# Expert stage of a two-layer backbone: the combined sums go through ACT and GpSimd into x, and the hidden activations are turned later

## The chip, the cores and the metric

One core of one Trainium2 chip. The metric is the device time in microseconds of one execution of the whole program. The names of the engines are PE (TensorE), DVE (VectorE), ACT (ScalarE), POOL (GpSimd) and SP (SyncE, which issues most of the transfers). SBUF is the on-chip memory, PSUM the memory into which PE writes.

## What is computed

One inference step with two trunk layers (DEPTH = 2) over 512 latent and 128 prompt tokens of width 1024. A layer has three token mixers with a gated merge, and then a mixture of 16 experts, which is where the change lies. In the reference:

```python
def expert_choice_ffn(h, w_router, w1, w3, w2):
    ...
    cap = CAPACITY_FACTOR * n_tok // N_EXPERTS
    xt = h.reshape(n_tok, D)
    aff = jax.nn.softmax((xt @ w_router).astype(jnp.float32), axis=-1)
    g, idx = lax.top_k(aff.T, cap)
    xe = xt[idx]
    hid = jax.nn.silu(jnp.einsum('ecd,edf->ecf', xe, w1)) * jnp.einsum('ecd,edf->ecf', xe, w3)
    ye = jnp.einsum('ecf,efd->ecd', hid, w2) * g[..., None].astype(h.dtype)
    out = jnp.zeros_like(xt).at[idx.reshape(-1)].add(ye.reshape(-1, D))
    return out.reshape(B, S, D)
...
    x = x + gate2 * expert_choice_ffn(h, p['w_router'], p['w_ff1'], p['w_ff3'], p['w_ff2'])
```

Each expert takes 64 latent and 16 prompt tokens. All is fp32. Its three weight matrices are 1024 x 1024, so the experts' weights are 16 x 12 MB per layer, and each is used once.

## The kernel before

**Chunks and units.** The experts run in eight pairs (A and B) per layer. The weights of a pair come in 24 chunks of 1 MB (128 x 4 x 512 fp32) into a ring of six slots. SP issues a load when `chunks_free` allows it (L747), and POOL counts that up (L847) once DVE has read the chunk. A chunk is worked on in two units, so a pair has 48 units, numbered 0 to 47. Eight units make a job, with its result in one of the two PSUM tensors `mm`: AF0, AF1, BF0, BF1 (hidden layer of A and B, two halves each), then AO and BO (the output products).

**Splitting a unit.** A product in fp32 is made as three products of rounded operands. For a unit, ACT rounds the weights (`w_hi<-ring`, in `hi_of_chunk`), DVE takes the rest (`w_lo<-ring,w_hi`, in `lo_of_chunk`), and PE makes two times three matmuls (in `job`, L1433). There are four buffers of `w_hi` and of `w_lo` (SPLITS = 4): ACT may begin on unit m when PE is through with unit m - 4 (`w_used`, or `mm_full` at a job's end).

**Order.** Each engine has its own program, written out by hand, tied by semaphores. ACT, DVE and POOL run over the chunks n of a pair and have other work put between them: DVE's `hidden(q)` (silu(w1 part) x w3 part, from `mm` and `tmp` to `hid`) comes after chunks 5, 9, 13 and 17; then PE turns the result (four transposes into `tp`, `turn_hidden`, L1445), ACT rounds it (`hi_of_hidden`) and DVE takes the rest (`lo_of_hidden`). `TURN_AT` gives the unit of PE ahead of which the turn stands, 10, 18, 26 and 34, and `after(unit)` the chunk after which ACT and DVE have their part. `SLOTS_AT` (20) and `ROWS_AT` (38) do the same for the tokens of the next pair: `find_slots` (L1377), POOL's `fetch` (an indirect transfer of rows, L840), and `turn_rows` (L1386). All turns share one PSUM tensor `tp`, handed on by `t_full` and `t_empty`.

**Combine and spread.** The output of a pair is added into x, scaled by gate2, during the next pair. Ahead of its units 8 to 15 PE makes one tile k of sums each, 128 x 512, by two matmuls into one of two PSUM tensors `oo` (`combine`, L1396). DVE adds tile k into x ahead of its own work for unit 12 + k (`spread`, by the helper on L1931), and gives `oo` back by `o_empty`. `combine` k + 2 waits for that. After the last pair all eight follow in a row.

**Other names.** `hot_t` is the matrix by which sums go to tokens; DVE rewrites it for the next combine after AF1's turn. `select` (DVE) compares positions for the pair after. L1492, L1923, L1927 and L1931 are the helpers `copy`, `tt`, `ts` and `stt`, so rows with these lines are told apart by their tiles. `stat<-stat,lam` is L2122, in the attention part: a two-input operation on one element per partition. L790, L792 and L796 are POOL's operations in that part.

Of the kernel before, what the change touches and what calls it, by code (L numbers as in the profile page):

```python
# [23 lines left out]
D = 1024  # L24
# [265 lines left out]
UNITS = 2  # L290
# [7 lines left out]
LAYER_USED = PAIRS * USED_PAIR  # L298
COMBINE_AT = JOB_UNITS

TURN_AT = [JOB_UNITS * (q + 1) + 2 for q in range(4)]
SLOTS_AT, ROWS_AT = TURN_AT[1] + 2, TURN_AT[3] + 4


def after(unit):
# [52 lines left out]
def build(nc, a):  # L358
    ctx = ExitStack()
    with ctx:  # L360
# [20 lines left out]
        def sem(name):  # L381
            return ctx.enter_context(nc.semaphore(name))
# [42 lines left out]
        def view(at, *shape):  # L425
# [5 lines left out]
            if len(shape) == 2:  # L431
# [108 lines left out]
        rows_stored, tokens_in, slots_ready, x_rows_in = (sem("rows_stored"), sem("tokens_in"), sem("slots_ready"),  # L540
                                                          sem("x_rows_in"))
        pool_waited = sem("pool_waited")
        xhi_ready, xe_ready = sem("xhi_ready"), sem("xe_ready")
        w_hi_ready, w_ready, w_used = sem("w_hi_ready"), sem("w_ready"), sem("w_used")
        silu_out, hid_ready, hid_hi_ready = sem("silu_out"), sem("hid_ready"), sem("hid_hi_ready")
# [90 lines left out]
        def pair_used(l, e, p):  # L636

            return l * LAYER_USED + e * USED_PAIR + (p - p // JOB_UNITS + 1)

        def t_bf0(last_pair):  # L640
            return T_BF0 - 1 if last_pair else T_BF0
# [120 lines left out]
        @block.gpsimd  # L762
        def _(pool):
            pool.sem_inc(chunks_free, RING)
            pool.sem_inc(small_free, 1)
            for s in (*mm_empty, t_empty, *o_empty):
                pool.sem_inc(s, 1)
            pool.sem_inc(ye_stored, 32)

            for l in range(DEPTH):  # L770
                def consumed(turn, n, e=None):

                    wait_mm_full(pool, l, turn, e)
                    pool.sem_inc(chunks_free, n)

                def ada_consumed(blocks):
                    for n in blocks:
                        pool.wait_ge(ada_full, n + 1)
                        pool.sem_inc(chunks_free, 2)

                if l == 0:
                    ada_consumed(range(ADA_FIRST))
                consumed(MM["da_v"] + TT - 1, 2)
                consumed(MM["da_q"] + 3, 2)
                consumed(DA_K[3], 2)

                def da_mix(i):
                    (p1, p2), _ = da_maps(i)
                    pool.wait_ge(da_weight, l * DA_N + i + 1)
                    pool.tensor_scalar(p2, p2, da_slot(i, "ratio"), 1.0, ALU.mult, ALU.mult)  # L790
                    pool.drain()
                    pool.tensor_tensor(p1, p1, p2, ALU.add).then_inc(p_mixed, 1)  # L792

                def da_square(t):
                    pool.wait_ge(da_kept, l * DA_N + DA_H * (t + 1))
                    pool.tensor_tensor(tmp[t % 2][:, 0:512], da_o[:, t, :], da_o[:, t, :], ALU.mult)\  # L796
                        .then_inc(da_squared, 1)

                for i in range(DA_N):
                    da_mix(i)  # L800
                    if i >= 5 and i % DA_H == 1:
                        da_square(i // DA_H - 1)
                da_square(PRT)
                for mb in range(2):
                    ada_consumed(gate_blocks(l, 0, mb))
                    consumed(MM["da_out"] + 8 * mb + 7, 3)
                consumed(MM["mla_in"] + 3, 2)
                consumed(SW_Q[3], 2)
                for i in range(MLA_N):

                    if i == MLA_N - TT:
                        consumed(mla_prep(MH - 1, 2), 2)
                    width = T if i % TT < LT else P
                    pool.wait_ge(ml_weight, l * MLA_N + i + 1)
                    pool.tensor_scalar(ml_p[i % 3][:, 0:width], ml_p[i % 3][:, 0:width],
                                       stat[:, 16 + i % 8:17 + i % 8], 1.0, ALU.mult, ALU.mult).then_inc(ml_scaled, 1)
                for mb in range(2):
                    ada_consumed(gate_blocks(l, 1, mb))
                    consumed(MM["mla_out"] + 8 * mb + 7, 3)
                consumed(SW_V, 2)  # L820

                for u in range(SW_PAIRS):

                    width = len(sw_tiles(u // SW_P)[0]) * P
                    pool.wait_ge(sw_weight, l * SW_PAIRS + u + 1)
                    for m in range(2):
                        last = pool.tensor_scalar(sw_p[u % 3][m][:, 0:width], sw_p[u % 3][m][:, 0:width],
                                                  sw_slot(u, "weight", m), 1.0, ALU.mult, ALU.mult)
                    last.then_inc(sw_scaled, 1)
                for mb in range(2):  # L830
                    ada_consumed(gate_blocks(l, 2, mb))
                    consumed(MM["sw_out"] + 8 * mb + 7, 3)
                consumed(MM["o"] + 3, 2)
                consumed(MM["o"] + 7, 2)


                def fetch(of):
                    pool.wait_ge(slots_ready, l * PAIRS + of + 1)
                    pool.sem_inc(pool_waited, 1)
                    pool.indirect_dma_start(x_rows, None, a["h_rows"], bass.IndirectOffsetOnAxis(slot_row, 0))\  # L840
                        .then_inc(x_rows_in, 16)

                def pair(e, last_pair=False):
                    for n in range(PAIR_CHUNKS):

                        pool.wait_ge(w_ready, pair_part(l, e, n * UNITS + UNITS - 1))
                        pool.sem_inc(chunks_free, 1)  # L847
                        if n == after(SLOTS_AT) + 1 and not last_pair:
                            fetch(e + 1)

                pool.wait_ge(rows_stored, 16 * LT * (l + 1))
                pool.dma_start(tokens, a["const"][:, CONST_COLS:]).then_inc(tokens_in, 16)
                fetch(0)
                with pool.Fori(0, PAIRS - 1) as e:
                    pair(e)
                pair(PAIRS - 1, True)

# [2 lines left out]
        def _(pe):  # L862
# [138 lines left out]
            for l in range(DEPTH):  # L1001
# [436 lines left out]
                def turn_hidden(q, turn, e):  # L1438

                    half, n = q // 2, q % 2  # L1440
                    rows_ = ROWS_OF[half]
                    pe.wait_ge(hid_ready, (l * PAIRS + e) * 4 + (q + 1))
                    wait_t_empty(pe, l, turn, e)
                    for k in range(4):
                        last = pe.transpose(tp[:, k * P:k * P + rows_],  # L1445
                                            hid[0:rows_, (4 * n + k) * P:(4 * n + k + 1) * P],
                                            ident[0:rows_, 0:rows_])
                    last.then_inc(t_full, 1)
# [41 lines left out]
        def _(act):  # L1490
# [76 lines left out]
            for l in range(DEPTH):  # L1567
# [237 lines left out]
                wait_t_full(act, l, TR["hot_p"])  # L1805
                copy(hotw_pt.rearrange("p g s -> p (g s)"), tp[:, 0:2 * P]).then_inc(t_empty, 1)

                def hi_of_chunk(n, e, last_pair=False):

                    i = AT[l, "pairs"] + n  # L1810
                    for u in range(UNITS):
                        m = UNITS * n + u
                        p = m - SPLITS
                        if p >= 0:

                            if p % JOB_UNITS == JOB_UNITS - 1:
                                wait_mm_full(act, l, job_turn(p // JOB_UNITS), e)
                            else:
# [44 lines left out]

                def pair(e, before=None, last_pair=False):
                    for n in range(2, PAIR_CHUNKS if last_pair else PAIR_CHUNKS + 2):
                        hi_of_chunk(n, e, last_pair)
                        if n == 2 and before is not None:
                            outputs(BO, before, False)
                        if n == 5:
# [51 lines left out]
        def _(dve):  # L1921
# [118 lines left out]
            for l in range(DEPTH):  # L2040
# [381 lines left out]
                        dve.drain()  # L2422
                        dve.sem_inc(ye_done, 1)

                def lo_of_chunk(n, e, before=None):
                    i = AT[l, "pairs"] + n
                    for u in range(UNITS):
                        m = UNITS * n + u
                        if before is not None and 0 <= m - SPLITS - COMBINE_AT < KT:
                            spread(m - SPLITS - COMBINE_AT, before)  # L2430
                        dve.wait_ge(w_hi_ready, pair_part(l, e, m))
                        tt(w_lo[m % SPLITS][:, :, :], chunk(i)[:, u * UK:(u + 1) * UK, :],
                           f(w_hi[m % SPLITS][:, :, :]), ALU.subtract).then_inc(w_ready, 1)
# [19 lines left out]
                def hidden(q, e, last_pair):  # L2453
# [3 lines left out]
                    n = q % 2  # L2457
                    dve.wait_ge(silu_out, (l * PAIRS + e) * 4 + (q + 1))
                    tt(hid[0:rows_, n * 512:(n + 1) * 512], mm[j % 2][0:rows_, 512:1024], tmp[n][0:rows_, 0:512],
                       ALU.mult).then_inc(mm_empty[j % 2], 1)  # L2460
                    dve.drain()  # L2461
                    dve.sem_inc(hid_ready, 1)

                def lo_of_hidden(q, e):
                    rows_ = ROWS_OF[q // 2]
# [5 lines left out]

                def pair(e, before=None, last_pair=False):
                    for n in range(2, PAIR_CHUNKS if last_pair else PAIR_CHUNKS + 2):
                        lo_of_chunk(n, e, before)
                        if n == 2 and before is not None:
                            outputs(BO, before, False)
                            dve.tensor_copy(aff_slot, aff_next)
# [6 lines left out]
                        if n == 9:  # L2484
                            hidden(AF1, e, last_pair)
                        if n == after(TURN_AT[AF1]):
                            ts(hot_t[:, :], tokens, slot_tok, ALU.is_equal)
                            lo_of_hidden(AF1, e)
                        if n == after(SLOTS_AT) and not last_pair:
# [31 lines left out]
                    pair(e, e - 1)  # L2521
                pair(PAIRS - 1, PAIRS - 2, True)
                outputs(BO, PAIRS - 1, True)
                for k in range(KT):
                    spread(k, PAIRS - 1)
                dve.drain()
# [51 lines left out]
```

## Time and profile before

| | us |
|---|---|
| timed runs, median of 3 (range) | 3376.07 (3367.52 to 3376.89) |
| profiled execution | 3354.95 |
| its span, first to last instruction | 3353.1 |
| PE busy | 2950.4 (88%) |
| DVE busy | 2173.1 (65%) |
| ACT busy | 1564.2 (47%) |
| POOL busy | 216.4 (6%) |

The mean granted TensorE clock is 0.951 of full speed. The experts of layer 0 run from 1022 us to about 1670, those of layer 1 from 2652 to about 3300. A busy PE counts matmuls from start to modelled end, and these overlap, so its share says less than the distance from one matmul to the next. In a row of a timeline the bracket tells how long the engine had been idle and what ended that; "DVEq" is DVE's instruction queue, such as a drain or a semaphore operation.

### The profile page before, as it was taken

To read this page: it belongs to the slowest core of one execution; us is meant where nothing else is said; L and a number is where in the kernel's file an instruction comes from. 1 tells how busy PE (TensorE), PEld (TensorE's weight loads), DVE (VectorE), ACT (ScalarE), POOL (GpSimd) and SP (SyncE) were. 2 spreads that over 40 slices of the span, in tenths; PEclk is the share of its full clock that TensorE was granted. 3 is DMA by queue.
4 is the path that set the end of the run, shared out by engine and by line. 5 is a ranking of instruction groups with operands and counts; after the bars stand their busy time and mean duration, and the time that the engine had idled before them with its cause. 6 is when DMAs were issued, how large, how long until landed. Compare 5 with 4: busy or idle time off the path is not lost.

```text
span 3353.1 us, 43928 instructions
## 1 busy us (share of the span) xinstructions
PE 2950.4 (88%) x15398; PEld 2141.2 (64%) x15398; DVE 2173.1 (65%) x3151; ACT 1564.2 (47%) x2258; POOL 216.4 (6%) x272
## 2 busy tenths in 40 slices
PE   6979988988977999999878898889799699999995
PEld 3767855766745666666656686567585366666663
DVE  3364445565447999999835553456762699999994
ACT  3161333132126777777543413321410477777773
POOL 0050011011000000000002300110200000000000
PEclk9989999999988999999988899999999699999996
DMA  7203200311416999999811031023013399999991
GB/s 268 82 1 111 77 27 26 127 65 51 157 72 243 327 330 321 327 330 326 284 65 57 26 137 52 1 76 114 28 38 112 117 334 321 327 326 326 330 335 55
DMA packets 280117, 564.13 MB, mean 168 GB/s; under 512 B 14040, under 2 KB 19872, under 8 KB 279328
## 3 DMA queue, kind: packets, MB, share of 16 engines
q1 hardware_dynamic: 273056, 543.33, 46.0%
q10 hardware_dynamic: 4448, 9.87, 0.8%
q0 software_dynamic: 2464, 8.91, 0.7%
q8 instruction: 97, 1.59, 0.2%
q14 instruction: 52, 0.43, 0.0%
HBM read 546.44 MB, written 15.63 MB: 168 GB/s over the span
## 4 chain that ended last, share of the span: by engine, by line
PE 65%; DVE 15%; ACT 7%; issue 5%; DVEq 4%; ACTq 2%; DMA 1%; POOL 0%; POOLq 0%; SPq 0%
PE mm L943 17%; PE mm L1433 17%; PE mm L878 11%; DVE w_lo L1923 6%; PE mm L1176 2%; DVEq L2461 2%; PE mm L975 2%; ACT w_hi L1492 2%; DVE x L1931 2%; ACTq L1861 2%; PE oo L1198 1%; PE oo L915 1%; DVE scratch L2112 1%; PE tp L1185 1%; DVE scratch L1923 1%
## 5 line engine op out<-in xcount | busy, mean ns | idle before, releaser
L1923 DVE TENSOR_TENSOR w_lo<-ring,w_hi 128x1024 fp32r<-128x1024 f32 x768 | 919.2, 1221 | 87.9 <-ACT w_hi L1492 57.7
L1492 ACT ACTIVATE w_hi<-ring 128x1024 fp32r<-128x1024 f32 x768 | 803.5, 1058 | 288.6 <-PE mm L1433 266.8
L1923 DVE TENSOR_TENSOR ring_lo<-ring,dw_hi 128x512 fp32r<-128x512 f32 (+1 forms) x168 | 113.6, 682 | 393.2 <-ACT dw_hi L1492 392.9
L1492 ACT ACTIVATE dw_hi<-ring 128x512 fp32r<-128x512 f32 (+1 forms) x168 | 103.5, 622 | 522.8 <-PE mm L943 518.3
L943 PE MATMUL mm<-h_hi,ring_lo 128*128 128x320 f32 (+1 forms) x1344 | 318.3, 318 | 20.9 <-DVE ring_lo L1923 14.4
L943 PE MATMUL mm<-h_lo,dw_hi 128*128 128x320 f32 (+1 forms) x1344 | 310.6, 313 | 0.0
L943 PE MATMUL mm<-h_hi,dw_hi 128*128 128x320 f32 (+1 forms) x1344 | 310.0, 312 | 0.0
L943 PEld LDWEIGHTS mm<-h_hi,ring_lo 128*128 128x128 f32 (+1 forms) x1344 | 225.0, 190 | 52.1 <-issue 37.3
L878 PE MATMUL mm<-scratch,ring 128*128 128x512 f32 (+3 forms) x896 | 256.5, 438 | 1.6 <-ACT scratch L1492 1.6
L943 PEld LDWEIGHTS mm<-h_lo,dw_hi 128*128 128x128 f32 (+1 forms) x1344 | 227.4, 190 | 1.1
L943 PEld LDWEIGHTS mm<-h_hi,dw_hi 128*128 128x128 f32 (+1 forms) x1344 | 226.6, 189 | 1.1
L1433 PE MATMUL mm<-w_lo,xa_hi 128*80 128x512 f32 x512 | 204.5, 399 | 15.5 <-DVE w_lo L1923 9.5
L878 PEld LDWEIGHTS mm<-scratch,ring 128*128 128x128 f32 (+1 forms) x896 | 140.9, 189 | 113.5 <-issue 111.0
L1433 PE MATMUL mm<-w_lo,xb_hi 128*128 128x512 f32 x512 | 203.8, 398 | 0.0
L1433 PE MATMUL mm<-w_hi,xa_lo 128*80 128x512 f32 x512 | 202.4, 395 | 0.0
L2008 DVE RECIPROCAL tmp<-tmp 128x640 f32<-128x640 f32 x48 | 199.3, 4153 | 3.9 <-issue 0.4
L1433 PE MATMUL mm<-w_hi,xa_hi 128*80 128x512 f32 x512 | 201.4, 393 | 0.0
L1433 PE MATMUL mm<-w_hi,xb_hi 128*128 128x512 f32 x512 | 199.7, 390 | 0.0
L1433 PE MATMUL mm<-w_hi,xb_lo 128*128 128x512 f32 x512 | 199.3, 389 | 0.0
L1492 ACT ACTIVATE scratch<-mm 16x1024 f32<-16x1024 f32 (+7 forms) x140 | 99.2, 718 | 149.2 <-PE mm L943 45.4
L878 PE MATMUL mm<-merged,ring 128*128 128x512 f32 (+1 forms) x512 | 138.8, 434 | 0.0
L1492 ACT ACTIVATE pt<-tp 128x640 f32<-128x640 f32 (+3 forms) x128 | 71.3, 557 | 106.6 <-PE tp L1271 63.3
(254 smaller groups left out, 4806.0 us busy)
## 6 DMA issues: line engine op xcount, KB each, us to landing
ring<-in_w_ff SPq DMA_DIRECT2D x384, 1024.0 KB, 6.1
ring<-in_w_ada SPq DMA_DIRECT2D x48, 1024.0 KB, 7.4
ring<-in_w_gate SPq DMA_DIRECT2D x24, 1024.0 KB, 5.7
ring<-in_w_in SPq DMA_DIRECT2D x16, 1024.0 KB, 9.4
ring<-in_w_o SPq DMA_DIRECT2D x8, 1024.0 KB, 7.5
x_spill<-x SPq DMA_DIRECT2D x2, 2560.0 KB, 12.5
ring<-in_w_br_da SPq DMA_DIRECT2D x4, 1024.0 KB, 6.3
ring<-in_w_br_mla SPq DMA_DIRECT2D x4, 1024.0 KB, 6.3
```

The costliest lines, as they stand in the source:

```text
L878: last = pe.matmul(out[:, lo:hi], lhs(n), rhs(n)[:, lo:hi], start=(n == 0), stop=(n == terms - 1))
L915: last = pe.matmul(oo[n % 2][32 * kk:32 * (kk + 1), 0:512], c_t[:, half * HALF + kk, :], chunk(i)[:, kk, :], start=(half == 0), stop=(half ...
L943: last = pe.matmul(out[0:width, lo:hi], w_, h_[:, k, lo:hi], start=(k == 0 and i == 0), stop=(k == KT - 1 and i == 2))
L975: last = pe.matmul(mm[j % 2][:, 0:width], h[:, k, t * P:(t + 1) * P], weight(c, k, c0, c0 + width), start=(k == 0), stop=(k == KT - 1))
L1176: last = pe.matmul(mm[j % 2][:, at:at + hi - lo], ml_q[hd % 2][0:MQ, t * P:(t + 1) * P], ml_k[hd % 2][0:MQ, lo:hi], start=True, stop=True)
L1433: last = pe.matmul(out[0:rows_, bank:bank + 512], a_[:, k, 0:rows_], b_[n % SPLITS][:, kk, :], start=(k == 0 and i == 0), stop=(k == KT - ...
L1492: return act.activation(out, in_, ACT.Copy, scale=scale)
L1861: act.drain()
L1923: return dve.tensor_tensor(out, in0, in1, op)
L1931: return dve.scalar_tensor_tensor(out=out, in0=in0, scalar=s, in1=in1, op0=op0, op1=op1)
L2008: dve.reciprocal(t_[:, :], t_[:, :])
L2461: dve.drain()
```

## The change

1. `spread` leaves DVE for the seven combines of a layer that fall into a following pair. ACT copies `oo`, scaled by gate2, from PSUM into one of four SBUF buffers (`spread_at`: `tmp[2]`, `rstd`, two parts of `merged`), ahead of its own wait for unit 12 + k. POOL then gives `oo` back and adds the buffer into x, ahead of its wait for that chunk. The eight adds after the last pair stay on DVE, which waits for POOL's first.
2. The hidden activations are turned two units later (12, 20, 28, 36), and `find_slots` with them (22); `turn_rows` stays at 38.
3. `hidden` no longer drains: it raises `hid_ready` itself, and PE gives `mm` back at the turn.
4. DVE waits for the last combine before it rewrites `hot_t`.

```diff
@@ constants
-TURN_AT = [JOB_UNITS * (q + 1) + 2 for q in range(4)]
-SLOTS_AT, ROWS_AT = TURN_AT[1] + 2, TURN_AT[3] + 4
+TURN_AT = [JOB_UNITS * (q + 1) + 4 for q in range(4)]
+SLOTS_AT, ROWS_AT = TURN_AT[1] + 2, TURN_AT[3] + 2
+SPREADS = (PAIRS - 1) * KT
+        def spread_at(k):
+            return (tmp[2][:, 0:NLAT], rstd[:, 0:NLAT], flat[:, D:D + NLAT], flat[:, D + NLAT:2 * D])[k % 4]
@@ pool
+            pool.sem_inc(spread_done, 4)
...
+                def spread(k, of):
+                    pool.wait_ge(spread_in, l * SPREADS + of * KT + (k + 1))
+                    pool.sem_inc(o_empty[(OO["pairs"] + k) % 2], 1)
+                    pool.tensor_tensor(x[:, k, 0:NLAT], x[:, k, 0:NLAT], spread_at(k), ALU.add).then_inc(spread_done, 1)
-                def pair(e, last_pair=False):
+                def pair(e, before=None, last_pair=False):
                     for n in range(PAIR_CHUNKS):
+                        if before is not None:
+                            for m in (UNITS * n, UNITS * n + 1):
+                                if 0 <= m - SPLITS - COMBINE_AT < KT:
+                                    spread(m - SPLITS - COMBINE_AT, before)
                         pool.wait_ge(w_ready, pair_part(l, e, n * UNITS + UNITS - 1))
                         pool.sem_inc(chunks_free, 1)
@@ tensor, turn_hidden
                     pe.wait_ge(hid_ready, (l * PAIRS + e) * 4 + (q + 1))
+                    pe.sem_inc(mm_empty[job_turn(q) % 2], 1)
                     wait_t_empty(pe, l, turn, e)
@@ scalar
+                def spread(k, of):
+                    j = OO["pairs"] + k
+                    act.wait_ge(spread_done, l * SPREADS + of * KT + (k + 1))
+                    wait_o_full(act, l, j, of)
+                    copy(spread_at(k), oo[j % 2][:, :], mod[:, 40 + k, 0:1]).then_inc(spread_in, 1)
@@ scalar, hi_of_chunk
+                            if before is not None and 0 <= p - COMBINE_AT < KT:
+                                spread(p - COMBINE_AT, before)
                             if p % JOB_UNITS == JOB_UNITS - 1:
@@ vector, lo_of_chunk
-                        if before is not None and 0 <= m - SPLITS - COMBINE_AT < KT:
-                            spread(m - SPLITS - COMBINE_AT, before)
                         dve.wait_ge(w_hi_ready, pair_part(l, e, m))
@@ vector, hidden
-                       ALU.mult).then_inc(mm_empty[j % 2], 1)
-                    dve.drain()
-                    dve.sem_inc(hid_ready, 1)
+                       ALU.mult).then_inc(hid_ready, 1)
@@ vector, pair
                         if n == after(TURN_AT[AF1]):
+                            if before is not None:
+                                wait_o_full(dve, l, OO["pairs"] + KT - 1, before)
                             ts(hot_t[:, :], tokens, slot_tok, ALU.is_equal)
@@ vector, after the last pair
+                dve.wait_ge(spread_done, (l + 1) * SPREADS + 4)
                 for k in range(KT):
                     spread(k, PAIRS - 1)
```

## Rows read from the trace of the kernel before

**Rows 1.** The page: busy tenths in 40 slices of 83.8 us each, DVE and DMA.
```profile
DVE  3364445565447999999835553456762699999994
...
DMA  7203200311416999999811031023013399999991
```

**Rows 2.** Busy time by window, one pair: length, engines (instructions), PEclk, DMA share, GB/s.
```profile
core 0: us, PE busy (x) PEld busy (x) DVE busy (x) ACT busy (x) POOL busy (x), PEclk, DMA share, GB/s
...
1298.04:1377.10 79.06, 74.69 (x338) 53.82 (x337) 72.42 (x79) 59.45 (x65) 1.31 (x1) 1.00 0.93 327
```

**Rows 3.** The page: DMA issues, the experts' weights: count, KB each, us to landing.
```profile
ring<-in_w_ff SPq DMA_DIRECT2D x384, 1024.0 KB, 6.1
```

**Rows 4.** Chain of waits, 1200 to 1300 us: start, length, what, so many matmuls.
```profile
1232.43 8.20 PE mm L1433 x36
```

**Rows 5.** Timeline of PE: start, length, operation, [idle before it and who ended it]; 1270 to 1340.
```profile
1274.69 0.45 PE L1433 MATMUL mm<-w_lo,xa_hi 128*80 128x512 f32 x1 [0.69 <-DVE w_lo L1923]
...
1282.07 0.50 PE L1396 MATMUL oo<-hot_t,ye_lo 128*128 128x512 f32 x1 [0.72 <-DVE x L1931]
...
1297.55 0.49 PE L1445 MATMUL tp<-const,scratch 80*128 80x80 f32 x4 [1.11 <-DVEq L2461]
...
1310.79 0.65 PE L1445 MATMUL tp<-const,scratch 128*128 128x128 f32 x4 [0.54 <-DVEq L2461]
...
1322.76 0.65 PE L1445 MATMUL tp<-const,scratch 128*128 128x128 f32 x4 [0.33 <-DVEq L2461]
...
1339.00 0.50 PE L1433 MATMUL mm<-w_lo,hidb_hi 128*128 128x512 f32 x1 [0.87 <-DVE w_lo L1923]
```

**Rows 6.** Timeline of PE in pair 0 of the first layer.
```profile
1048.80 0.50 PE L1445 MATMUL tp<-const,scratch 80*128 80x80 f32 x4 [1.06 <-DVEq L2461]
...
1060.81 0.49 PE L1445 MATMUL tp<-const,scratch 80*128 80x80 f32 x4 [0.52 <-DVEq L2461]
```

**Rows 7.** Groups by shape, 1040 to 1640: count, busy us, mean ns, idle us before.
```profile
L1492 ACT ACTIVATE w_hi<-ring 128x1024 fp32r<-128x1024 f32 x369 | 386.5, 1058 | 136.9 <-PE mm L1433 126.5 <-issue 9.6
...
L1931 DVE SCALAR_TENSOR_TENSOR x<-oo,mod,x 128x512 f32<-128x512 f32 x56 | 41.6, 744 | 1.5 <-issue 1.4
...
L1841 ACT ACTIVATE tmp<-mm 128x512 f32<-128x512 f32 x16 | 9.3, 579 | 0.0
...
L1377 PEld LDWEIGHTS tp<-scratch 128*128 128x128 f32 x56 | 6.8, 191 | 3.3 <-issue 3.3
```

**Rows 8.** Timeline of DVE, from unit 6's w_lo to AF1's hida_lo.
```profile
1273.41 6.90 DVE L1923 TENSOR_TENSOR w_lo<-ring,w_hi 128x1024 fp32r<-128x1024 f32 x6 [0.20 <-ACT w_hi L1492]
...
1292.43 0.76 DVE L1923 TENSOR_TENSOR scratch<-const,pos_t 128x256 f32<-128x256 f32 x2
...
1295.56 1.22 DVE L1923 TENSOR_TENSOR w_lo<-ring,w_hi 128x1024 fp32r<-128x1024 f32 x1
...
1299.87 0.48 DVE L1927 TENSOR_SCALAR hot_t<-merged,stat 128x512 fp32r<-128x512 f32 x1
...
1300.26 0.48 DVE L1923 TENSOR_TENSOR hida_lo<-tp,hida_hi 128x320 fp32r<-128x320 f32 x1
```

**Rows 9.** Groups by shape, POOL, whole run: two-input operations.
```profile
L792 POOL TENSOR_TENSOR scratch<-scratch 128x640 f32<-128x640 f32 x32 | 49.5, 1546 | 5.8 <-issue 1.7
...
L796 POOL TENSOR_TENSOR tmp<-scratch 128x512 f32<-128x512 f32 x10 | 10.4, 1039 | 6.6 <-DVEq L2131 6.5
...
L792 POOL TENSOR_TENSOR scratch<-scratch 128x128 f32<-128x128 f32 x8 | 3.6, 454 | 1.2
```

**Rows 10.** Timeline of POOL and DVE side by side, 196 to 199 and 1876 to 1878.
```profile
196.38 1.54 POOL L792 TENSOR_TENSOR scratch<-scratch 128x640 f32<-128x640 f32 x1
...
196.39 0.82 DVE L2112 CUSTOM_DVE_ANT_0 scratch<-mm,const 128x640 f32<-128x640 f32 x1 [0.23 <-issue]
...
198.67 0.22 DVE L1931 SCALAR_TENSOR_TENSOR stat<-stat,lam 128x1 f32<-128x1 f32 x1
...
1876.69 1.04 POOL L796 TENSOR_TENSOR tmp<-scratch 128x512 f32<-128x512 f32 x1 [1.17 <-DVEq L2131]
...
1876.95 0.80 DVE L1931 SCALAR_TENSOR_TENSOR stat<-stat,lam 128x1 f32<-128x1 f32 x1
```

More of the change, by code:

```diff
@@ L542, in build @@
         pool_waited = sem("pool_waited")
+        spread_in, spread_done = sem("spread_in"), sem("spread_done")
         xhi_ready, xe_ready = sem("xhi_ready"), sem("xe_ready")
@@ L853, in _ @@
                 fetch(0)
-                with pool.Fori(0, PAIRS - 1) as e:
-                    pair(e)
-                pair(PAIRS - 1, True)
+                pair(0)
+                with pool.Fori(1, PAIRS - 1) as e:
+                    pair(e, e - 1)
+                pair(PAIRS - 1, PAIRS - 2, True)
         @block.tensor
@@ L1806, in _, with hi_of_chunk @@
                 copy(hotw_pt.rearrange("p g s -> p (g s)"), tp[:, 0:2 * P]).then_inc(t_empty, 1)
-                def hi_of_chunk(n, e, last_pair=False):
+                def spread(k, of):
[3 more added lines that the diff above has]
+                    copy(spread_at(k), oo[j % 2][:, :], mod[:, 40 + k, 0:1]).then_inc(spread_in, 1)
+                def hi_of_chunk(n, e, before=None):
                     i = AT[l, "pairs"] + n
@@ L1865, in pair @@
                     for n in range(2, PAIR_CHUNKS if last_pair else PAIR_CHUNKS + 2):
-                        hi_of_chunk(n, e, last_pair)
+                        hi_of_chunk(n, e, before)
                         if n == 2 and before is not None:
@@ L2423, in outputs, with lo_of_chunk @@
                         dve.sem_inc(ye_done, 1)
-                def lo_of_chunk(n, e, before=None):
+                def lo_of_chunk(n, e):
                     i = AT[l, "pairs"] + n
@@ L2473, in pair @@
                     for n in range(2, PAIR_CHUNKS if last_pair else PAIR_CHUNKS + 2):
-                        lo_of_chunk(n, e, before)
+                        lo_of_chunk(n, e)
                         if n == 2 and before is not None:
```

## Prediction

> **What bounds the kernel now.** The page is read first for its slices. In the two stretches where the experts run, DMA and DVE both show 9 almost throughout, so neither can be ruled out by eye [rows 1]. The busy time by window is read next. Over one whole pair of experts, 79.06 us, PE is busy 74.7 us, DVE 72.4, ACT 59.5, POOL 1.3, and the DMA share is 0.93 [rows 2]. A pair moves 24 chunks, and each lands 6.1 us after its issue (median) [rows 3], while the ring of six chunks turns in 6/24 x 79.06 = 19.8 us: the transfers have slack, and what is left is PE and DVE.
>
> The timeline of PE shows who holds whom. The chain of waits gives the pace of an undisturbed PE: 36 matmuls in 8.20 us, 0.228 each [rows 4]. A unit of six is 1.37 us, and 1.82 with the two matmuls of combine. So a pair's 288 + 16 matmuls cost 69.3 us. Of the other 9.8 us some 4 are transposes and find_slots, and the rest are stalls, the same six in each pair [rows 5] and small ones. I give each as the idle time printed plus some 0.15 to 0.25 us of restart: unit 4, 0.9 (DVE late behind the output of the pair before); combine 2, 1.0 (waits for DVE's add into x); AF1's transposes, 1.35; BF0's, 0.7; BF1's, 0.5 (these three wait for the drain behind `hidden`); unit 44, 1.1 (ACT and DVE late behind outputs). In pair 0 there is no combine, and AF0's and AF1's transposes wait 1.2 and 0.7 us [rows 6].
>
> **The change part by part.**
>
> *DVE loses eight adds.* Each was 0.744 us [rows 7], so 8 x 0.744 = 6.0 us of 72.4 per pair. In that phase DVE is PE's neighbour: 1.15 us for a w_lo back to back (6.90 for six [rows 8]) + 0.74 for an add = 1.9 at most, and PE needs 1.82. It is DVE's insertions there (hidden, hida_lo, the selection) that make combine 2 and AF1 late.
>
> *ACT gains eight copies.* The nearest row is the silu of the same 128x512 PSUM operand, 0.58 us [rows 7]: 4.6 us per pair onto 59.5. 1.06 for a w_hi + 0.58 = 1.64 is under 1.82, and the copy stands before the wait for w_used, in ACT's idle time. Cost nothing; if PE came faster than 1.64 per unit it would cost up to 0.3 us per unit.
>
> *Turns move two units later, and the drain behind hidden goes.* hid_ready is then 2 x 1.37 = 2.7 us less urgent, more than any of the waits. AF0 to BF1 stop stalling. find_slots moves with AF1's turn (its distance stays 2), and POOL's fetch with it by one chunk: 16 units less two remain before turn_rows, and 20 us hide it. turn_rows stays, now 2 units behind BF1's turn: the distance that find_slots has before, where PE idles 3.3/7 = 0.5 us [rows 7] with one operation more of DVE in between (hot_t, 0.48). I put 0 (range 0 to 0.5). mm_empty is given by PE at the turn, four units before its next use: nothing.
>
> *The wait of POOL.* Each add stands ahead of POOL's wait for a chunk, and behind the previous one. SP's loads are queued behind chunks_free. A delay there of a few us lies inside the ring's 19.8 - 6.1 us. But o_empty for combine 4 now comes only after POOL has passed w_ready of unit 13: PE waits for POOL, and POOL for DVE.
>
> *The adds themselves on POOL.* Not shown before. By L792, which adds two different operands: 640 elements 1.546 us, 128 elements 0.454, so 2.13 ns per element, and 512 give 1.27 us. L796 with one operand twice took 1.04 [rows 9]. I take 1.27, as the adds have two operands; ends 1.04 and 1.55. Eight are 10.2 us per pair.
>
> *What they do to DVE.* This decides the case. At 1876.95 DVE begins `stat<-stat,lam` 128x1, which has two tensor inputs in SBUF. It takes 0.80 us instead of 0.22, and ends at 1877.75; POOL's add ran from 1876.69 to 1877.73. An operation of DVE with one input in PSUM, begun at 196.39 under a POOL add that began at 196.38, takes its usual 0.82 [rows 10]. So a DVE operation with two SBUF inputs stands still until POOL's is over, and the others do not. w_lo<-ring,w_hi has two SBUF inputs, 48 times per pair; the add taken from DVE had one. No row shows a POOL operation started under such a DVE operation. Its wait is between 0 and 1.22 us. What is held by one until its last moment I read as held by one at a time, both ways, and take the upper end. The Trainium skill says the same (SBUF — State Buffer, Who interferes with whom): a DVE instruction with two SBUF inputs contends with a GpSimd instruction that reads SBUF, and the later of the two fully blocks; by it the sum below stays as it is, at 3395. The trace agrees for DVE behind POOL (0.80 against 0.22 us); no row shows the other direction.
>
> *The sum for one pair with combine* (clock of the pair shown, DVE in [rows 8]). The first POOL add can begin at 1280.7, when lo of unit 11 is done (1273.41 + 6.90 = 1280.3, + 0.4 for copy and semaphores). From then one of the two always has work: 8 w_lo x 1.18 = 9.4, 8 adds x 1.27 = 10.2, the selection 0.7 (two SBUF inputs too): 20.3 us, to 1301.0; w_lo of unit 19 is done 1.2 earlier, 1299.8, against 1295.56 + 1.22 = 1296.8 before. Then four w_lo for units 20 to 23, 4.7, and hot_t with hida_lo, 0.8: 1306.5. find_slots waits for that hida_lo, now two units later. Before, hida_lo ended at 1300.26 + 0.48 = 1300.74; two units of PE later is 1303.5. Delay 1306.5 - 1303.5 = +3.0 us, which holds all that combine 2 and AF1's turn gave back. BF0 and BF1 give 0.7 + 0.5 = 1.2. Net +1.8 us per pair.
> Pairs with combine: 14. Pair 0, twice: 1.2 + 0.7 + 0.7 + 0.5 = 3.1 us gained, 6.2 in all. Total 14 x 1.8 - 6.2 = +19 us. The profiled execution was 3354.95 us (span 3353.1), so 3374; it lay 21 us below the median 3376.07 of the timed runs, and on that the same 19 us make 3395. In shares, +0.6%; ±0.3% (10 us) is about what a measurement of this kernel can tell from no change.
> Bounds: adds of 1.04 take 8 x 0.23 = 1.8 off a pair: -6 us in all, 3370. A handover of 0.1 us on each of 16 changes, or adds of 1.47, add 1.6: 14 x 3.4 - 6.2 = +41, 3417.
>
> **The rivals.**
> 1. *Serialised, as summed*: 3395, own range 3387 to 3420. For it: [rows 10]. Against: only small DVE operations show it. Chance 0.50.
> 2. *Serialised, but balanced*: w_lo holds the port shorter than its 1.22 us, or adds are near 1.04, so a pair changes by 0 to +1.0 us: 3370 to 3384, take 3376. Chance 0.19.
> 3. *Faster*: POOL does not wait for a running w_lo. Then an add starts beside one, is over within it or 0.3 us after, and DVE's lateness stays under the slack of the four buffers: 3 x 1.82 - 2.9 = 2.5 us (2.9 is 1.06 + 1.22 and three semaphores of some 0.2). All four stalls go: 14 x (1.0 + 1.35 + 0.7 + 0.5) + 6.2 = 56 us; -56 gives 3320, or 3325 with 0.3 per pair lost at combine 4. The same time if w_lo should not stand still at all. It decides from the point where w_lo plus the lateness of the add is under 1.82 us per unit. DMA would then run at 327 x 79.06 / 75.5 = 342 GB/s, a share of 0.97: still possible. Chance 0.24.
> 4. *Worse*: DVE always goes first and POOL adds only in its gaps. combine k + 2 waits for POOL to reach add k, chunks are freed late, and ACT's copy k waits for add k - 4. Price: five adds of 1.27 in gaps of 0.6 per unit are 10 units instead of 7, 3 x 1.8 = 5.5 us per pair: 14 x 5.5 - 14 x 1.2 - 6 = +54, 3430 and up. Chance 0.07.
> That the change does not shorten DVE cannot be: the adds are off it.
>
> The predicted time is rival 1's, 3395. The range 3318 to 3420 takes in rival 3, 2 and 1, and leaves out rival 4 and the tails. Faster 0.24, within 0.3% 0.19, slower 0.57.
>
> **What the profile after would show.** Step by step: x<-x adds on POOL, 112, mean 1.27 us (longer where they wait for DVE). Mean w_lo over 1.22, and in combine's phase maxima near 2.4: the clearest sign of serialising. Period of a pair 81 us, against 75.5 in rival 3. PE's waits: L1445 <- DVEq gone; PE oo <- POOL at combine 4, about 1 us; PE tp L1377 (find_slots) waiting up to 3 us for hida_lo. In pair 0 no stall at the turns. ACT's copy near 0.58. It would be wrong if w_lo keeps 1.22 throughout, or if POOL's adds show a time of about 1.3 with w_lo unchanged beside them; and the size is wrong if the lateness is absorbed before unit 22.

## The result and the profile after

| | before | after |
|---|---|---|
| timed runs, median (range), us | 3373.02 (3367.52 to 3378.14), 8 runs | 3384.55 (3379.29 to 3389.11), 8 runs |
| ratio after to before | | 1.0036, interval 1.0023 to 1.0048 |
| span of the profiled execution | 3353.1 | 3380.1 |
| POOL busy | 216.4 | 438.0 |
| ACT busy | 1564.2 | 1622.7 |
| DVE busy | 2173.1 | 2200.5 |

The change is 12 us slower. One execution of the kernel with find_slots two units further (below) took 12326 us and is left out of its ratio. DVE gave 112 adds away and is busy for 27 us more. The groups by shape of the page after say why. First w_lo, then POOL's three groups of adds (the buffer is named by the tile it lies in); columns as in [rows 7].

```profile
L1951 DVE TENSOR_TENSOR w_lo<-ring,w_hi 128x1024 fp32r<-128x1024 f32 x768 | 991.5, 1328 | 75.3 <-ACT w_hi L1511 58.2
```

```profile
L854 POOL TENSOR_TENSOR x<-x,merged 128x512 f32<-128x512 f32 x56 | 102.5, 1851 | 19.8 <-DVE w_lo L1951 19.8
L854 POOL TENSOR_TENSOR x<-x,rstd 128x512 f32<-128x512 f32 x28 | 63.8, 2279 | 0.0
L854 POOL TENSOR_TENSOR x<-x,tmp 128x512 f32<-128x512 f32 x28 | 50.0, 1784 | 642.5 <-DVE w_lo L1951 642.5
```

w_lo has gone from 919.2 us in all to 991.5, and one of them took up to 2.32 us, where 1.228 was the longest before. An add of POOL took 1.8 to 2.3 us on average. The timelines of both engines in the middle of a combine phase show the same seen close; first DVE, then POOL.

```profile
1291.32 0.69 DVE L1951 TENSOR_TENSOR scratch<-mm,tmp 80x512 f32<-80x512 f32 x1
...
1301.86 2.24 DVE L1951 TENSOR_TENSOR w_lo<-ring,w_hi 128x1024 fp32r<-128x1024 f32 x1
1304.02 2.96 DVE L1951 TENSOR_TENSOR scratch<-const,pos_t 128x256 f32<-128x256 f32 x2
1306.90 2.28 DVE L1951 TENSOR_TENSOR w_lo<-ring,w_hi 128x1024 fp32r<-128x1024 f32 x1
```

```profile
1291.64 1.29 POOL L854 TENSOR_TENSOR x<-x,tmp 128x512 f32<-128x512 f32 x1 [46.10 <-DVE w_lo L1951]
...
1300.74 2.27 POOL L854 TENSOR_TENSOR x<-x,tmp 128x512 f32<-128x512 f32 x1
1302.97 2.27 POOL L854 TENSOR_TENSOR x<-x,rstd 128x512 f32<-128x512 f32 x1
1305.21 2.89 POOL L854 TENSOR_TENSOR x<-x,merged 128x512 f32<-128x512 f32 x2
```

The first add, begun with DVE in an operation that reads PSUM, takes 1.29 us. Those that have a w_lo within them end 2.24 us apart, and the last two, beside the two operations of the selection, take 2.89 us together: the two engines take turns. At the end of the phase DVE is late, and PE waits (timeline of PE, one pair; columns as in [rows 5]):

```profile
1296.51 0.50 PE L1414 MATMUL oo<-hot_t,ye_lo 128*128 128x512 f32 x1 [0.52 <-POOLq L853]
...
1309.24 0.80 PE L1451 MATMUL mm<-w_lo,xb_hi 128*128 128x512 f32 x1 [2.12 <-DVE w_lo L1951]
1309.83 0.63 PE L1451 MATMUL mm<-w_hi,xb_lo 128*128 128x512 f32 x1
1310.26 0.63 PE L1451 MATMUL mm<-w_hi,xb_hi 128*128 128x512 f32 x1
...
1317.09 1.05 PE L1395 MATMUL tp<-scratch 128*128 x8 [0.24 <-DVE hida_lo L1951]
...
1351.24 0.50 PE L1451 MATMUL mm<-w_lo,hidb_hi 128*128 128x512 f32 x1 [0.88 <-DVE w_lo L1951]
...
1365.99 0.46 PE L1451 MATMUL mm<-w_lo,xa_hi 128*80 128x512 f32 x1 [0.69 <-DVE w_lo L1951]
```

Of the six stalls of [rows 5] the last and the first stay (0.88 and 0.69; the first stands at unit 6, which the prediction calls unit 4). The four at combine 2 and the turns are gone. In their place stand combine 4 behind POOL (0.52), unit 18 behind w_lo (2.12), and find_slots behind hida_lo. The matmuls after 1309.24 start 0.43 us apart instead of 0.23: the granted clock has fallen. The windows show it, and the period of four pairs, two of each layer (columns as in [rows 2]):

```profile
1302.00:1308.00 6.00, 5.11 (x23) 3.62 (x21) 6.00 (x4) 5.38 (x7) 6.00 (x4) 1.00 0.77 290
1308.00:1312.00 4.00, 2.76 (x7) 2.19 (x8) 4.00 (x5) 0.21 (x1) 0.10 (x1) 0.64 0.24 67
...
1243.81:1324.31 80.50, 76.05 (x339) 55.33 (x338) 74.82 (x71) 63.83 (x74) 16.77 (x10) 0.98 0.90 321
1324.31:1404.38 80.07, 75.87 (x338) 55.18 (x337) 74.80 (x71) 63.58 (x74) 16.77 (x10) 0.98 0.91 322
2918.69:2998.36 79.67, 74.31 (x337) 53.99 (x336) 74.37 (x72) 63.60 (x73) 16.76 (x9) 1.00 0.91 324
2998.36:3079.62 81.26, 75.93 (x337) 55.12 (x336) 74.41 (x72) 63.62 (x73) 16.77 (x9) 0.98 0.90 318
```

Pairs 1 to 6 of a layer take 79.6 to 81.3 us, 80.5 on average, against 79.06 in [rows 2]. All twelve have the stall of 2.1 us at unit 18, and they are of three kinds. In six the clock falls behind that stall; PE then waits 0.25 us or less at find_slots, and the pair takes 80.0 to 80.5 us. In four it falls behind find_slots, after a wait of 1.1 us there: 81.2 to 81.3. In two it does not fall, with the same wait of 1.1: 79.6 and 79.7.

**Where the 27 us between the two spans belong.** From the first w_lo to the last, the expert stage took 631.7 and 632.9 us before, 637.1 and 638.9 after: 11.4 us more in both layers, the size of the timed difference. It is made up of +17.1 us in pairs 1 to 6 of both layers, -4.0 in the two pairs 0, which have no combine, and -1.7 in the two last pairs, which have no selection and no find_slots. By the three kinds of pairs, the 17.1 us are 12 x (79.65 - 79.07) = 7.0 us of waits and 10.1 us of slow clock (6.4 in the four pairs with the fall behind find_slots, and 3.6 in the six others). The other 15 us lie in the attention parts. The first experiment looks whether these belong to the change.

### The profile page after: what moved, and what is told of

Read it like the earlier page. It is cut to its first block, busy times and chain, and to the rows that moved or that the text cites. A ratio compares the mean times of both kernels' runs of the same rounds, so it can differ in the third digit from the quotient of the medians.

```text
span 3380.1 us, 44353 instructions
## 1 busy us (share of the span) xinstructions
PE 2976.7 (88%) x15398; PEld 2166.4 (64%) x15398; DVE 2200.5 (65%) x3039; ACT 1622.7 (48%) x2370; POOL 438.0 (13%) x384
## 4 chain that ended last, share of the span: by engine, by line
PE 68%; DVE 15%; issue 7%; ACT 6%; ACTq 2%; DVEq 1%; DMA 1%; POOL 0%; POOLq 0%; SPq 0%
PE mm L1451 19%; PE mm L961 17%; PE mm L896 11%; DVE w_lo L1951 6%; PE mm L1194 2%; PE mm L993 2%; DVE scratch L1951 2%; ACTq L1889 2%; ACT w_hi L1511 2%; PE oo L1216 1%; PE oo L933 1%; DVE scratch L2140 1%; PE tp L1203 1%; PE oo L1303 1%; DVE tmp L1951 1%
## 5 line engine op out<-in xcount | busy, mean ns | idle before, releaser
L1951 DVE TENSOR_TENSOR w_lo<-ring,w_hi 128x1024 fp32r<-128x1024 f32 x768 | 991.5, 1328 | 75.3 <-ACT w_hi L1511 58.2
L1451 PE MATMUL mm<-w_lo,xb_hi 128*128 128x512 f32 x512 | 212.0, 414 | 26.4 <-DVE w_lo L1951 26.4
L822 POOL TENSOR_SCALAR scratch<-scratch,stat 128x640 f32<-128x640 f32 (+1 forms) x80 | 57.2, 715 | 619.9 <-DVE stat L2232 619.9
```

Of the source, the lines that this page charges most:

```text
L1451: last = pe.matmul(out[0:rows_, bank:bank + 512], a_[:, k, 0:rows_], b_[n % SPLITS][:, kk, :], start=(k == 0 and i == 0), stop=(k == KT - ...
L1951: return dve.tensor_tensor(out, in0, in1, op)
```

## The experiments

Theory L: POOL's adds and DVE's w_lo exclude one another, in both directions, and that costs more than the later turns give back. Rival M: the new chain of semaphores through ACT and POOL, or ACT's eight copies, cost it. Theory C, formed on the trace after: the fall of the clock behind the stall at unit 18 is a part of the loss.

### The kernel before, once more

> The kernel before, unchanged, for a second profile. The two profiled executions differ by 27 us, the timed medians by 12, and the expert stages of the two traces by 11.4 (5.4 in layer 0, 6.0 in layer 1). Theory: the other 15 us are in the attention parts, where the clock of single executions differs, and have nothing to do with the change: this profile shows its first w_lo at 1031 to 1033 us (1022.0 in the first profile), an expert stage of 632 us again, a span of 3365 to 3370, ratio 1.000. Rival: the changed program is slower there too; then this one again begins its experts at 1022.

Ratio 0.9994 (0.9981 to 1.0007), span 3375.9. Its w_lo in the two layers (count, ns min/median/max, first and last start):

```profile
L1923 DVE TENSOR_TENSOR w_lo<-ring,w_hi x384: 1211/1224/1228, 1032.5 to 1665.5; 128x1024 fp32r<-128x1024 f32 x192
L1923 DVE TENSOR_TENSOR w_lo<-ring,w_hi x384: 1211/1224/1228, 2674.4 to 3307.4; 128x1024 fp32r<-128x1024 f32 x192
```

The experts begin at 1032.5 and take 633.0 us twice, although the span is 23 us longer than in the first profile. The mean clock was 0.943 then and 0.951 in the first. So the attention parts differ from one execution to another, and the change costs what its expert stages show: 4 and 6 us.

### The turns alone

```diff
-TURN_AT = [JOB_UNITS * (q + 1) + 2 for q in range(4)]
-SLOTS_AT, ROWS_AT = TURN_AT[1] + 2, TURN_AT[3] + 4
+TURN_AT = [JOB_UNITS * (q + 1) + 4 for q in range(4)]
+SLOTS_AT, ROWS_AT = TURN_AT[1] + 2, TURN_AT[3] + 2
...
+                    pe.sem_inc(mm_empty[job_turn(q) % 2], 1)
...
-                       ALU.mult).then_inc(mm_empty[j % 2], 1)
-                    dve.drain()
-                    dve.sem_inc(hid_ready, 1)
+                       ALU.mult).then_inc(hid_ready, 1)
```

> The kernel before with parts 2 and 3 of the change alone: turns and find_slots two units later, no drain in hidden, mm given back by PE. The adds stay on DVE. Theory L (the changed kernel lost its gain because POOL's adds and DVE's w_lo exclude one another, and because PE's longer stalls let its clock fall): no stall at the turns, combine 2 still waits (1.0 us), so a pair becomes 76.5 to 77.0 us instead of 79.05, w_lo stays at 1.22, no fall of the clock; 14 x 2.2 + 6 = 37 us less, ratio 0.989 (0.986 to 0.992). Rival M (the turns only move DVE's lateness, the stalls return behind them): under 10 us, ratio 0.997 to 1.000.

Ratio 0.9884 (0.9863 to 0.9906): 39 us less. One pair, and the waits that are left in the combine phase:

```profile
1227.64:1304.39 76.75, 74.13 (x338) 54.04 (x337) 71.69 (x79) 59.11 (x66) 1.72 (x2) 1.00 0.97 339
```

```profile
1276.38 0.50 PE L1396 MATMUL oo<-hot_t,ye_lo 128*128 128x512 f32 x1 [0.39 <-DVE x L1932]
...
1297.17 1.05 PE L1377 MATMUL tp<-scratch 128*128 x8 [0.65 <-DVE hida_lo L1924]
```

The later turns, together with the missing drain, are a gain by themselves; the adds on DVE cost PE 0.39 us per pair. What makes the change slower is all in the other part. Which of the two, places or drain, gives how much of the 39 us was not taken apart.

### The adds on POOL alone

The changed kernel with the diff above undone.

> The changed kernel with parts 2 and 3 undone: adds on POOL, turns at their old places, with the drain. Theory L: the phase ends as late as in the changed kernel (w_lo mean 1.33, up to 2.32 us), and the stalls of BF0 (0.7), BF1 (0.5) are back, as are those of pair 0: 14 x 1.2 + 6 = 23 us or more above the changed kernel, so +35 us on the kernel before, ratio 1.010 (1.007 to 1.016), with the clock's fall once in each pair. Rival M: taking the adds off DVE alone gains what combine 2 and AF1's turn waited, 14 x 2.3 = 32 us less, ratio 0.990.

Ratio 1.0183 (1.0164 to 1.0201): the sign of theory L, but 61 us instead of 35. A wait of one pair, and two pairs:

```profile
1322.18 0.79 PE L1463 MATMUL tp<-const,scratch 80*128 80x80 f32 x4 [4.54 <-DVEq L2486]
```

```profile
1250.73:1334.98 84.25, 77.02 (x338) 55.85 (x337) 75.48 (x71) 63.78 (x74) 16.74 (x9) 0.96 0.87 307
1334.98:1418.19 83.21, 75.95 (x338) 55.06 (x337) 75.50 (x71) 63.75 (x74) 16.75 (x9) 0.98 0.89 310
```

I had reckoned only with what the turns' own stalls cost before. But DVE now comes to `hidden` of AF1 late by its turns with POOL, and PE stands 4.54 us ahead of a turn at unit 18. The clock falls behind that in every pair with a combine, once (pairs of 83.1 to 83.3 us) or for twice as long (84.1 to 84.6). With the turn two units later the same lateness costs 2.1 us at unit 18 and up to 1.1 at find_slots. The two parts together give +0.36%, their own effects +1.83% and -1.16% add up to +0.67%.

### A fill in place of the add

```diff
-                    pool.tensor_tensor(x[:, k, 0:NLAT], x[:, k, 0:NLAT], spread_at(k), ALU.add).then_inc(spread_done, 1)
+                    pool.memset(spread_at(k), 0.0).then_inc(spread_done, 1)
```

> The changed kernel with POOL's add replaced by a fill of the buffer, an operation that writes SBUF and reads nothing; the sums of the pairs 0 to 6 are not added into x. All semaphores, ACT's copies and the order stay. Theory L: w_lo stays at 1.22 (mean and maximum), all stalls at combine 2 and the turns are gone, a pair takes 75.5 to 76 us, the clock does not fall, ratio 0.984 (0.981 to 0.987). Rival M (the chain ACT, POOL, PE of semaphores, or ACT's eight copies, cost the gain): a pair stays at 80.3, ratio 1.003.

Ratio 0.9837 (0.9807 to 0.9868). POOL's largest group, w_lo, and one pair:

```profile
L854 POOL MEMSET merged<- 128x512 f32 x56 | 29.5, 527 | 69.1 <-DVE w_lo L1951 55.3 <-ACT merged L1511 13.8
```

```profile
L1951 DVE TENSOR_TENSOR w_lo<-ring,w_hi x768: 1205/1224/1228, 1031.8 to 3253.6; 128x1024 fp32r<-128x1024 f32 x192
```

```profile
1234.40:1309.96 75.56, 73.72 (x338) 54.17 (x337) 67.18 (x71) 63.48 (x74) 5.95 (x9) 1.00 0.97 342
```

Every semaphore and every copy is there, and a pair takes 75.56 us with w_lo at its old time. Rival M falls. But a fill is also shorter (0.53 us) than an add, so this run alone does not tell reading from length; for w_lo's duration the next one does.

### A scaling in place of the add

```diff
-                    pool.tensor_tensor(x[:, k, 0:NLAT], x[:, k, 0:NLAT], spread_at(k), ALU.add).then_inc(spread_done, 1)
+                    pool.tensor_scalar(spread_at(k), spread_at(k), 1.0, 1.0, ALU.mult, ALU.mult).then_inc(spread_done, 1)
```

> The changed kernel with POOL's add replaced by a scaling of the buffer in place, which reads SBUF, one input, 0.69 us instead of 1.27; the sums of the pairs 0 to 6 are not added into x. Theory L: w_lo waits for it too, mean about 1.27, maximum about 1.9. Per unit 1.15 + 0.69 is near PE's 1.82, so lateness stays inside the buffers: no fall of the clock, a pair 76 to 77 us, ratio 0.986 (0.983 to 0.991). Rival M: ratio 1.003 as for the changed kernel. If scaling gives the time of the fill exactly and w_lo keeps 1.22, only operations with two inputs on POOL exclude DVE's.

Ratio 0.9843 (0.9817 to 0.9869). POOL's groups and w_lo:

```profile
L854 POOL TENSOR_SCALAR rstd<-rstd 128x512 f32<-128x512 f32 x28 | 30.2, 1078 | 13.6 <-ACT rstd L1511 13.6
L854 POOL TENSOR_SCALAR tmp<-tmp 128x512 f32<-128x512 f32 x28 | 17.3, 618 | 661.4 <-DVE w_lo L1951 661.4
```

```profile
L1951 DVE TENSOR_TENSOR w_lo<-ring,w_hi x768: 1204/1224/1659, 1032.6 to 3254.0; 128x1024 fp32r<-128x1024 f32 x192
```

The exclusion is there: 1.08 us where w_lo is in the way, 0.62 where it isn't, and a w_lo of up to 1.66. It costs no time: w_lo and the scaling, 1.2 + 0.5 to 0.6, fit into PE's 1.82 us per unit. So it is not the exclusion as such that costs, but the sum with w_lo where it is over PE's step. An operation as long as the add that reads nothing was not run; that it would cost nothing is argued, from its 1.3 us against 1.82, not shown.

### PE kept busy through its wait

```diff
+                        if before is not None and n == 18:
+                            wait_t_empty(pe, l, T_AF1, e)
+                            for _ in range(6):
+                                pe.matmul(tp[:, 0:512], ye_hi[:, 0:P], hot_t[:, :], start=True, stop=True)
                         pe.wait_ge(w_ready, pair_part(l, e, n))
```

> The changed kernel with six matmuls more per pair, ahead of PE's wait for unit 18, where it idles 2.1 us: they read ye_hi and hot_t and write into the free tp, and nothing uses them. Theory C (a part of the loss is TensorE's clock, which falls for 3.4 us once in each pair behind that stall, and six matmuls at half speed instead of 0.23 us each cost 1.6 us): the clock stays at 1.00 through the expert stage, a pair takes 78.7 to 78.9 us instead of 80.4, 14 x 1.6 = 22 us less than the changed kernel, ratio 0.997 (0.995 to 0.999). Rival (the slow clock lies beside DVE's lateness, which sets the time anyway): a pair stays at 80.0 to 80.4, ratio 1.003, clock or no clock.

Ratio 1.0036 (1.0023 to 1.0048), no gain. The stall at unit 18 is short and without a fall of the clock, but the wait at find_slots is 1.0 to 1.1 us in all of pairs 1 to 6, and in six of the twelve the clock falls behind that:

```profile
1307.83 0.50 PE L1455 MATMUL mm<-w_lo,xb_hi 128*128 128x512 f32 x1 [0.80 <-DVE w_lo L1955]
1315.01 1.05 PE L1395 MATMUL tp<-scratch 128*128 x8 [1.04 <-DVE hida_lo L1955]
```

```profile
1242.57:1323.80 81.23, 77.26 (x344) 56.22 (x343) 74.60 (x71) 63.55 (x74) 16.81 (x10) 0.98 0.89 318
```

In the changed kernel the slow matmuls after unit 18 are over when PE comes to find_slots, and it waits 0.24 us there for DVE; here it is early and waits 1.04. The slow clock at unit 18 lay in part beside DVE's lateness: the six pairs of the changed kernel with it took 0.3 to 0.8 us more than the two without a fall. Where the clock falls behind find_slots, nothing covers it: such pairs take 81.3 us here, those without a fall 79.7. So the run moved the fall and did not take it away (6 x 1.6 = 10 us of slow clock here, 10.1 us in the changed kernel), and it is no test of the clock as a whole. Theory C had put 1.6 us per pair at unit 18, and it is 3.6 us in all there. But the slow clock at both places together is the larger part of what the changed kernel loses in pairs 1 to 6 (10.1 of 17.1 us), as its own pairs with and without a fall show.

### find_slots two units further

```diff
-SLOTS_AT, ROWS_AT = TURN_AT[1] + 2, TURN_AT[3] + 2
+SLOTS_AT, ROWS_AT = TURN_AT[1] + 4, TURN_AT[3] + 2
```

> The changed kernel with find_slots at unit 24 instead of 22 (and POOL's fetch one chunk later). By the lock's account PE waits at find_slots 1.1 to 1.4 us only because it stands close behind hida_lo; two units later DVE's lateness is made good at 0.2 us per unit, so some 0.8 of the 1.2 us go: a pair 79.6, 11 us less than the changed kernel, ratio 1.000 (0.998 to 1.002). The stall at unit 18 and the clock's fall behind it stay. Rival (the lateness moves on to the next wait): a pair stays at 80.4, ratio 1.003.

Ratio 0.9955 (0.9938 to 0.9973): 15 us under the kernel before, 27 under the changed one where I had put 11.

```profile
1386.68 0.50 PE L1451 MATMUL mm<-w_lo,xb_hi 128*128 128x512 f32 x1 [2.11 <-DVE w_lo L1951]
```

```profile
1324.43:1402.73 78.30, 74.06 (x338) 54.08 (x337) 74.36 (x71) 63.70 (x74) 16.06 (x9) 1.00 0.93 329
```

The 2.11 us at unit 18 stay; the wait at find_slots is gone and none takes its place; and in ten of pairs 1 to 6 the clock stays at 1.00 (78.3 to 78.4 us), although PE idled as long at unit 18. In the other two it falls behind unit 18, and they take 79.9: with no wait behind it to take it up, a fall costs 1.6 us there too. The two expert stages are 24.0 us shorter than in the changed kernel, and some 7 us of that are clock (2 x 1.6 of slow clock against 10.1). I had let 0.4 us of the lateness come back, and had left the clock out. One line beside the adds decides whether the change is slower or faster than the kernel before.

### Every second add on DVE

```diff
-SPREADS = (PAIRS - 1) * KT
+SPREADS = (PAIRS - 1) * KT // 2
...
+                    if k % 2 == 0:
+                        return
...
+                        if before is not None and 0 <= k < KT and k % 2 == 0:
+                            spread(k, before)
                         dve.wait_ge(w_hi_ready, pair_part(l, e, m))
```

> The changed kernel with every second add (even k) back on DVE from PSUM; the odd ones go by ACT and POOL. Theory L: the locked time in the phase is 8 x 1.15 + 4 x 1.1 = 13.6, and DVE's own adds 4 x 0.66 lie beside POOL's, so per two units DVE needs 2.3 + 1.1 + 0.66 = 4.1 us at most, 3.6 where an add of DVE runs under one of POOL, against PE's 3.64: lateness under 2 us, no fall of the clock. A pair 76 to 77 us, ratio 0.988 (0.984 to 0.992), w_lo mean about 1.26. Rival (any add on POOL costs a fixed wait through the chain of semaphores): a pair 78 us or more, ratio over 0.993.

Ratio 0.9936 (0.9921 to 0.9951), outside what I had put for theory L (0.984 to 0.992) and where the rival had put it. Its pairs 1 to 6 are of two kinds, 78.9 to 79.1 us (six) and 77.3 to 77.5 (six). First DVE and then POOL at the first add:

```profile
1286.70 0.74 DVE L1963 SCALAR_TENSOR_TENSOR x<-oo,mod,x 128x512 f32<-128x512 f32 x1
1287.36 2.35 DVE L1955 TENSOR_TENSOR w_lo<-ring,w_hi 128x1024 fp32r<-128x1024 f32 x2
```

```profile
1287.14 3.73 POOL L856 TENSOR_TENSOR x<-x,tmp 128x512 f32<-128x512 f32 x1 [46.65 <-ACT tmp L1513]
```

```profile
1308.97 1.05 PE L1397 MATMUL tp<-scratch 128*128 x8 [1.09 <-DVE hida_lo L1955]
```

The stall at unit 18 is gone, so halving the adds did what the lock's account says. What I had not in the sum is find_slots: 1.0 to 1.1 us, in pairs of both kinds; in those of 79 us the clock falls behind it, which costs 1.6 us again. The rival's cause, a fixed wait through the semaphores, is refuted by the fill. The run shows too that turns are not always taken in the order of the recorded starts: this add began 0.22 us ahead of the first w_lo and waited for two in a row, 3.73 us.

### Adds on DVE, the rest further apart

The turns alone, and beside them:

```diff
-COMBINE_AT = JOB_UNITS
+COMBINE_AT = JOB_UNITS + 2
...
+SLOTS_AT, ROWS_AT = TURN_AT[1] + 4, TURN_AT[3] + 2
```

> Adds on DVE as in the kernel before, turns and missing drain as in the change, find_slots at unit 24, and the combines ahead of units 10 to 17 instead of 8 to 15, further behind the output of the pair before. No lock can play. In the trace of the kernel with the turns alone PE still waits 0.4 us at combine 2 and 0.65 to 0.85 at find_slots; both should go: a pair 75.5 to 75.8 us instead of 76.7, ratio 0.984 (0.981 to 0.987). If DVE's 72 us per pair are by now what sets the time, it stays at 76.5, ratio 0.988.

Ratio 0.9846 (0.9831 to 0.9861), 3317.43 us: 52 us under the kernel before, the lowest median of those that compute everything. A pair and the one wait left in the combine phase:

```profile
1237.03:1312.96 75.93, 74.03 (x338) 53.97 (x337) 71.80 (x79) 59.24 (x66) 1.23 (x1) 1.00 0.95 340
```

```profile
1293.50 0.50 PE L1396 MATMUL oo<-hot_t,ye_lo 128*128 128x512 f32 x1 [0.31 <-DVE x L1932]
```

The combines yet two units further:

```diff
-COMBINE_AT = JOB_UNITS + 2
+COMBINE_AT = JOB_UNITS + 4
```

> The last kernel (adds on DVE, turns later, find_slots at 24) with the combines ahead of units 12 to 19 instead of 10 to 17. In its trace PE waits 0.3 us at one combine, behind the hidden activations of AF0; two units later DVE is through with them, so that wait may go: a pair 75.6 instead of 75.9, ratio 0.983 (0.981 to 0.986). Rival: the adds then meet AF1's turn, hot_t and hida_lo, and a wait of over 0.5 us comes at find_slots or at unit 20: a pair 76.5 or more, ratio 0.988.

Ratio 0.9864 (0.9844 to 0.9884), a pair 76.11 us, the wait still 0.26: neither the gain nor the loss that I had put. It moves with the adds.

## Why the prediction came out as it did

The direction was right, and the exclusion was at work; the size was 19 us where 12 were measured. That the two are this near is in part luck: the waits that the prediction summed cost far less than it put, and a fall of the clock that it did not have made up for most of that. By this trace's waits alone the expert stages would have come out 1.3 us longer (7.0 - 4.0 - 1.7; an estimate from one execution), which is no change that the timed runs could tell.

- *DVE stands still under POOL's add*: right, from rows of 0.8 us against 0.22 [rows 10]. w_lo shows 2.24 to 2.32 us.
- *POOL waits for a running w_lo too*: no row of before had this, and rival 3 (0.24) lived on it. Right: 2.27 us in the changed kernel, 1.08 against 0.62 in the scaling.
- *An add is 1.27 us*: right for one that nothing holds (1.29). *Adds and w_lo sum up to 20.3 us*: this term was too large. Taking turns they come every 2.24 us, not every 1.18 + 1.27 = 2.45. Add 1 began at 1291.64 and the last ended at 1305.21 + 2.89 = 1308.1, 16.5 us, where the sum had 20.3. Six w_lo and not eight were done within it (2 x 1.18 = 2.4 us), and the six turns were 0.2 us shorter (1.3).
- *Where PE waits*: the places were combine 4 (about 1 us) and find_slots (up to 3 us). The trace shows 0.52 at combine 4, 2.1 at unit 18, which was not forecast, and up to 1.1 at find_slots. The selection, held twice (2.96 us for two of 0.4), brings the stall forward to unit 18: in the last pair of a layer, which has none, PE waits 0.2 and 0.3 us at units 19 and 20 instead.
- *Turns of BF0 and BF1*: right; none of these waits is in the trace, and the kernel with the turns alone gave 39 us where the expectation had 37.
- *Pair 0*: 3.1 us were put, and 1.8 and 2.2 came. The stalls at the turns are gone, but find_slots has a wait of 0.5 us in their place.
- *14 pairs with a combine*: the two last ones do not lose +1.8 us but gain 0.8 each, as they have no selection and no find_slots.
- *ACT's copies cost nothing*: right by the fill, though one takes 0.67 us and not 0.58.
- *The net per pair*: +1.8 was put, +1.4 came (80.5 against 79.07, pairs 1 to 6). Only 0.6 of that are waits, the term that was mis-sized; 0.8 is the fall of the clock, which was not in the sum.
- *The chunks' frees through POOL*: right as far as the trace tells, a transfer still lands in 6.2 us (6.1 before, [rows 3]), and PE's waits are for DVE and POOL.

Not settled: why the clock falls behind the stall at unit 18 in half of the changed kernel's pairs 1 to 6, behind find_slots in a third and not at all in two, with the same waits; and why it falls in only two of the twelve with find_slots two units further, where PE idles as long at unit 18. How often it fell in the timed executions other than the profiled one was not looked at.

## What to carry to other kernels

Before work goes from DVE to POOL, look at the operands of what DVE does beside it: if these have two SBUF inputs and POOL reads SBUF, the two durations nearly add up, and what counts is whether their sum fits into the step of the engine that sets the pace. Here it did for a scaling (about 1.8 us against 1.82) and did not for an add (2.24). A wait of PE can cost more than its idle time: compare pairs with the same waits and another clock before putting a price on it. And take a change apart before judging it: its less visible half, later places for the turns and a drain less, was worth 39 us alone, and the adds on POOL alone cost 61.

## What was not expected of the hardware

- Alternating operations of DVE and POOL that exclude one another cost 2.24 us per pair of them, 0.25 us less than the 1.22 + 1.27 that they take alone.
- POOL isn't always next in turn: one add stood through two w_lo that followed without a gap, 3.73 us.
- A fill on POOL, which reads nothing, left w_lo at 1.205 to 1.228 us in all of 768.
- PE's clock went from 2.4 to 1.2 GHz for some seven to nine matmuls (0.43 us apart instead of 0.23) behind waits of 2.1 us at unit 18, and of 1.0 to 1.1 us at find_slots; it did not do so behind each of them. It cost 1.6 us of a pair where no other engine was late behind it (three kernels: 81.3 against 79.7, 79.9 against 78.3, 79.0 against 77.4), and 0.3 to 0.8 where DVE was.
